# A hybrid decoder layer on one core: squares behind the rounded tiles of x, heads' rows by DMA and one transpose, the normalised input split in place

## The reference, cut to what matters

```
h = rmsnorm(x) * g_mix
proj = h @ w_in + b_in      # cv, cg (512 each), q, k, v, og (1024 each), ig, fg (4 each), ga, gb (1024 each)
a = cv * sigmoid(cg);  c = silu(layernorm(depthwise31(a)));  conv_out = c @ w_co
log_i = ig;  log_f = log_sigmoid(fg)
# mLSTM per head (4 heads of 256), by chunks, with a running maximum m:
#   bcum = cumsum(log_f); D = bcum[t] - bcum[s] + log_i[s]; m_t = max(bcum + m, max D)
#   weights exp(D - m_t), inter exp(bcum + m - m_t), states decayed by exp(bcum_end + m - m_new)
mlstm = sigmoid(og) * headnorm(h_heads) * g_mn
x = x + (sigmoid(ga) * conv_out + sigmoid(gb) * mlstm) @ w_o
x = x + (silu(gt) * up) @ w_fo      # gt, up = split(rmsnorm(x) * g_ffn @ w_fi)
y = rmsnorm(x) * g_final            # and the new conv rows and states C, n, m
```

## Time and profile before

| | us |
|---|---|
| median of 3 runs | 962.69 |
| lowest, highest | 961.84, 964.0 |
| the profiled execution, its own time | 963.81 |
| its span, first to last instruction | 962.3 |
| TensorE busy in it | 940.0 |
| VectorE, ScalarE, GpSimd busy | 774.7, 466.4, 120.2 |
| mean granted TensorE clock | 0.989 of full speed |

### The profile page before, as it was taken

One profiled execution on the slowest core, in us unless ns is written; L12 is line 12 of the kernel. 1 busy time (PEld: TensorE's weight loads), 2 busy tenths in 40 slices (PEclk: granted clock), 3 DMA queues, 4 the chain that ended last, 5 costly groups with the idle time before them and its releaser, 6 DMA issues.

```text
span 962.3 us, 18468 instructions
## 1 busy us (share of the span) xinstructions
PE 940.0 (98%) x6846; PEld 914.1 (95%) x6846; DVE 774.7 (81%) x1231; ACT 466.4 (48%) x686; POOL 120.2 (12%) x117
## 2 busy tenths in 40 slices
PE   6999999999999999999999999999999999999996
PEld 5999999999999999999999999999999999999995
DVE  6875979698779859796445559899888998989996
ACT  5743454246344524453743344455445554555573
POOL 4133051015003300510123000000000000000001
PEclk9988999999999999999999999999999999999998
DMA  5225212620442152123242222222232223233122
GB/s 194 86 66 175 72 41 100 219 87 23 156 161 66 55 219 88 44 87 138 97 162 67 86 88 88 88 89 90 96 121 91 88 66 111 90 108 109 48 86 98
DMA packets 22067, 97.26 MB, mean 101 GB/s; under 512 B 2704, under 2 KB 4880, under 8 KB 17648
## 3 DMA queue, kind: packets, MB, share of 16 engines
q1 hardware_dynamic: 19504, 77.13, 24.3%
q0 software_dynamic: 1680, 18.42, 5.2%
q10 hardware_dynamic: 816, 0.88, 0.3%
HBM read 84.03 MB, written 12.39 MB: 100 GB/s over the span
## 4 chain that ended last, share of the span: by engine, by line
PE 81%; DVE 9%; issue 3%; ACT 3%; DMA 1%; POOL 1%; SPq 0%; POOLq 0%; DVEq 0%; ACTq 0%
PE ps L1286 43%; PE ps L1558 25%; PE ps L1531 3%; PE ps L1386 2%; PE ps L1410 2%; PE ps L1458 2%; DMA raw<-w_fp_in 1%; PE ps L1396 1%; DVE main L2156 1%; PE ps L1467 1%; DVE hf L1743 1%; PE ps L1443 1%; PE ps L1447 0%; DVE main L2189 0%; PE ps L1445 0%
## 5 line engine op out<-in xcount | busy, mean ns | idle before, releaser
L1286 PE MATMUL ps<-h_hi,w_hi 128*128 128x288 f32 x896 | 194.9, 299 | 0.0
L1286 PE MATMUL ps<-h_lo,w_hi 128*128 128x288 f32 x896 | 192.7, 297 | 0.0
L1286 PE MATMUL ps<-h_hi,w_lo 128*128 128x288 f32 x896 | 192.5, 297 | 0.0
L785 ACT ACTIVATE w_hi<-raw 128x1024 fp32r<-128x1024 f32 x76 | 80.3, 1057 | 186.7 <-PE ps L1286 184.0
L1286 PEld LDWEIGHTS ps<-h_hi,w_hi 128*128 128x128 f32 x896 | 144.3, 190 | 2.1 <-issue 1.4
L1286 PEld LDWEIGHTS ps<-h_hi,w_lo 128*128 128x128 f32 x896 | 145.2, 190 | 0.0
L1286 PEld LDWEIGHTS ps<-h_lo,w_hi 128*128 128x128 f32 x896 | 145.1, 190 | 0.0
L1681 DVE TENSOR_TENSOR w_lo<-raw,w_hi 128x1024 fp32r<-128x1024 f32 x76 | 94.2, 1239 | 58.0 <-ACT w_hi L785 57.8
L1896 DVE SCALAR_TENSOR_TENSOR conv<-a_p,vec,conv x120 | 97.6, 813 | 0.2
L721 POOL TENSOR_TENSOR cs_lo<-cs,cs_hi 128x512 fp32r<-128x512 f32 x32 | 42.3, 1356 | 166.4 <-ACT cs_hi L921 166.4
L1558 PE MATMUL ps<-cols_b,late 128*128 128x288 f32 x432 | 62.8, 294 | 0.0
(11 more groups left out here) (360 smaller groups left out, 1886.9 us busy)
## 6 DMA issues: line engine op xcount, KB each, us to landing
raw<-w_head_in SPq DMA_DIRECT2D x40, 512.0 KB, 3.5
raw<-w_fp_in SPq DMA_DIRECT2D x18, 1024.0 KB, 4.8
cs<-st_c_in POOLq DMA_DIRECT2D x4, 2048.0 KB, 9.3
c_s_out<-cs POOLq DMA_DIRECT2D x4, 2048.0 KB, 7.7
raw<-w_fo_in SPq DMA_DIRECT2D x8, 1024.0 KB, 4.8
x<-xT_in SPq DMA_DIRECT2D x16, 288.0 KB, 4.2
raw<-w_cgcv_in SPq DMA_DIRECT2D x8, 512.0 KB, 4.7
raw<-w_ga_in SPq DMA_DIRECT2D x8, 512.0 KB, 3.6
```

The costliest lines, as they stand in the source:

```text
L785: act.activation(w_hi[:, s, :], raw[:, s, :], ACT.Copy).then_inc(hi_ready, 1)
L1286: last = pe.matmul(ps[:, 2 * s + b, 0:HALF], wt[:, w, k * P:k * P + P], src[:, k, b * HALF:b * HALF + HALF], start=(k == 0 and wt is w_hi ...
```

## The change

1. **Squares.** All eight tiles of x are rounded first; the eight squares follow, to `xsq`, which lies over the space of `h_hi` and `h_lo`, and VectorE alone adds them. The first weights are loaded ahead of the second tile of x. `mean` moves from the end of unit 0 to the middle of unit 1. The first table that ScalarE loads is that of the square root.
2. **First pair.** ScalarE copies units 0 and 1 out of PSUM unscaled (`unscaled`); VectorE scales them in place later (`scaled_there`). The split of unit 2's weights stands ahead of the reciprocal.
3. **Heads' rows.** `nrow`, `drow` and `rows` go to DRAM by GpSimd's DMAs. `nrow` and `drow` come back spread over all partitions, to `negm` and `dec`; `rows` comes back as `items`, 88 partitions of 128, and one transpose in the middle of unit 7 turns it. `sel`, `keep_negm` and TensorE's small products go.
4. **Normalised input.** VectorE writes `hn` (all eight tiles, in the space of `h_lo`) and subtracts in place to `h_lo`. TensorE waits for each tile of it inside the head's first unit.

```diff
@@ names and places @@
+        xsq = nc.alloc_sbuf_tensor_at("xsq", [P, KT, T], F32, offset=place[0])
         h_hi = sb("h_hi", [KT, T], F32R)
+        hn = nc.alloc_sbuf_tensor_at("hn", [P, KT, T], F32, offset=place[0])
         h_lo = sb("h_lo", [KT, T], F32R)
-        sel = sb("sel", [NH, P], parts=NH)
+        items = sb("items", P, parts=NH * NI)
@@ SyncE @@
-            sp.dma_start(x[:, 1, :], xT[:, 1, :]).then_inc(x_loaded[1], 16)
             sp.dma_start(raw[:, 0, :], w_cgcv[0]).then_inc(raw_loaded[0], 16)
-            for k in range(2, KT):
+            for k in range(1, KT):
@@ GpSimd @@
-            for k in range(KT):
-                pool.wait_ge(hhi_ready, k + 1)
-                pool.tensor_tensor(h_lo[:, k, :], hf[:, k % 2, :], h_hi[:, k, :].bitcast(F32), ALU.subtract)\
-                    .then_inc(hlo_ready, 1)
-
-            pool.wait_ge(mrow_ready, 1)
+            pool.wait_ge(mrow_ready, 2)
+            pool.dma_start(nrow_d, nrow[:, :]).then_inc(negm_spread, 16)
             pool.dma_start(m_p, mrow[:, TP - 1:TP]).then_inc(out_stored, 16)
+            pool.wait_ge(negm_spread, 16)
+            pool.dma_start(negm[:, :, :], nrow_d.partition_broadcast(P)).then_inc(negm_spread, 16)
             pool.wait_ge(exps_in, 1)
             pool.dma_start(m_s, mend[:, :]).then_inc(out_stored, 16)
+            pool.wait_ge(exps_out, 4)
+            pool.dma_start(rows_d.rearrange("(h n) p -> h (n p)", h=NH), rows[:, :]).then_inc(items_moved, 16)
+            pool.dma_start(drow_d, drow[:, :]).then_inc(negm_spread, 16)
+            pool.wait_ge(items_moved, 16)
+            pool.dma_start(items[:, :], rows_d).then_inc(items_moved, 16)
+            pool.wait_ge(negm_spread, 48)
+            pool.dma_start(dec[:, :, :], drow_d.partition_broadcast(P)).then_inc(negm_spread, 16)
+            pool.wait_ge(negm_spread, 64)
@@ ScalarE @@
-                if k >= 2:
-                    act.wait_ge(sq_added_odd if k % 2 else sq_added, k // 2)
-                act.activation(tmp[:, k % 2, :], x[:, k, :], ACT.Square).then_inc(sq_ready, 1)
...
+            for k in range(KT):
+                act.activation(xsq[:, k, :], x[:, k, :], ACT.Square).then_inc(sq_ready, 1)
+
+            def unscaled(u):
+
+                act.wait_ge(unit_done, u + 1)
+                act.activation(halves(conv if u else tmp, 0), slot(u), ACT.Copy).then_inc(slot_read[u], 1)
...
-            deviation(3, sum_done, 1)
-
             act.wait_ge(gates_done, 1)
...
             split_hi(1, 0)
+            unscaled(0)
+            deviation(3, sum_done, 1)
+            unscaled(1)
+            split_hi(1, 1)
             conv_gate(0)
-            split_hi(1, 1)
@@ TensorE @@
-            pe.wait_ge(slot_read[2], 1)
-            pe.wait_ge(exps_out, 4)
-            pe.wait_ge(masks_ready, 2)
-            for n in range(NI):
-                pe.transpose(ps[:, 4, n * NH:n * NH + NH], rows[:, n * P:n * P + P], ident[0:NH, 0:NH])
...
-            pe.wait_ge(hlo_ready, KT)
+            def turn_items(k):
+                if k == KT // 2:
+                    pe.wait_ge(slot_read[2], 1)
+                    pe.wait_ge(items_moved, 32)
+                    pe.wait_ge(masks_ready, 2)
+                    pe.transpose(ps[:, 4, 0:NH * NI], items[:, :], ident[0:NH * NI, 0:NH * NI]).then_inc(turned, 1)
+
+            unit(N_A - 1, 1, 1, C_B - 1, xg_hi, xg_lo, KT, ready=turn_items)
...
+                head_unit(0, beside=lambda k: pe.wait_ge(hlo_ready, k + 1))
@@ VectorE @@
-                if k % 2 == 0:
-                    add_square(k)
-            dve.wait_ge(sq_added_odd, KT // 2)
-            dve.wait_ge(sq_added, KT // 2)
-            dve.tensor_tensor(acc[:, :], acc[:, :], hf[:, 0, :], ALU.add).then_inc(sq_added, 1)
             split_lo(1, 1)
+            for k in range(1, KT):
+                add_square(k)
...
+            split_lo(2, 0)
             rstd(3, 1, 1)
             dve.wait_ge(rs_ready, 1)
-            scaled(0)
-            split_lo(2, 0)
-            scaled(1)
+            scaled_there(0)
             split_lo(3, 1)
+            scaled_there(1)
...
+            def normalised_lo(k):
+
+                dve.wait_ge(hhi_ready, k + 1)
+                dve.tensor_tensor(h_lo[:, k, :], hn[:, k, :], h_hi[:, k, :].bitcast(F32), ALU.subtract)\
+                    .then_inc(hlo_ready, 1)
```

More of the change, by code:

```diff
@@ L853, in _ @@
             conv_gate(2)
-            for k in range(5):
+            for k in range(4):
                 norm_hi(k)
             split_hi(3, 1)
-            for k in range(5, KT):
+            for k in range(4, KT):
                 norm_hi(k)
-            split_hi(4, 0)
+                if k == KT - 3:
+                    split_hi(4, 0)
             conv_gate(3)
-            def keep_negm(h):
-                act.wait_ge(negm_spread, h + 1)
-                act.activation(halves(negm, h), slot(3 - h % 2), ACT.Copy).then_inc(slot_read[3 - h % 2], 1)
-            keep_negm(0)
             split_hi(4, 1)
-            for h in range(1, NH):
-                keep_negm(h)
             def evac_bias(h, j, dst):
@@ L1325, in _ @@
             unit(0, 0, 0, START, xg_hi, xg_lo, KT, ready=beside_first_unit)
-            unit(1, 1, 1, START, xg_hi, xg_lo, KT)
+            unit(1, 1, 1, START, xg_hi, xg_lo, KT, ready=beside_second_unit)
             with pe.Fori(1, N_A // 2 - 1) as i:
@@ L1330, in _ @@
             unit(N_A - 2, 0, 0, C_B - 1, xg_hi, xg_lo, KT)
-            pe.wait_ge(slot_read[2], 1)
-            pe.wait_ge(exps_out, 4)
-            pe.wait_ge(masks_ready, 2)
-            for n in range(NI):
-                pe.transpose(ps[:, 4, n * NH:n * NH + NH], rows[:, n * P:n * P + P], ident[0:NH, 0:NH])
-            for h in range(NH):
-                last = pe.matmul(ps[:, 5, h * SB:h * SB + SB], sel[:, h, :], drow[:, :], start=True, stop=True)
-            last.then_inc(turned, 1)
-            for h in range(NH):
-                s = 3 - h % 2
-                pe.wait_ge(slot_read[s], (1 if s == 3 else 2) + h // 2)
-                for b in range(2):
-                    last = pe.matmul(ps[:, 2 * s + b, 0:HALF], sel[:, h, :], nrow[:, b * HALF:b * HALF + HALF],
-                                     start=True, stop=True)
-                last.then_inc(negm_spread, 1)
-                if h == 0:
-                    unit(N_A - 1, 1, 1, C_B - 1, xg_hi, xg_lo, KT)
-            pe.wait_ge(hlo_ready, KT)
+            def turn_items(k):
+                if k == KT // 2:
+                    pe.wait_ge(slot_read[2], 1)
[3 more added lines that the diff above has]
+            unit(N_A - 1, 1, 1, C_B - 1, xg_hi, xg_lo, KT, ready=turn_items)
             with pe.Fori(0, NH) as h:
@@ L1375, in read @@
                         pe.wait_ge(dve_read, h * DVE_USES + (READER[:k].count("dve") + START + 1))
-                for j in range(6):
+                head_unit(0, beside=lambda k: pe.wait_ge(hlo_ready, k + 1))
+                for j in range(1, 6):
                     head_unit(j)
@@ L1836, in _ @@
             split_lo(6, 0)
-            for k in range(5):
+            for k in range(4):
                 normalised(k)
+                if k:
+                    normalised_lo(k - 1)
             scaled(5)
+            normalised_lo(3)
             split_lo(7, 1)
+            for k in range(4, KT):
+                normalised(k)
+                if k == KT - 2:
+                    scaled(6)
+                    split_lo(8, 0)
+                if k > 4:
+                    normalised_lo(k - 1)
+            normalised_lo(KT - 1)
             conv_input(2)
-            for k in range(5, KT):
-                normalised(k)
-            scaled(6)
-            split_lo(8, 0)
             dve.wait_ge(turned, 1)
-            steps.on(dve.tensor_copy(dec[:, :, :].rearrange("p h b -> p (h b)"), ps[:, 5, 0:NH * SB]))
-            dve.tensor_copy(cols[:, :, :].rearrange("p i h -> p (i h)"), ps[:, 4, 0:NI * NH]).then_inc(slot_read[2], 1)
+            dve.tensor_copy(cols[:, :, :], ps[:, 4, 0:NH * NI].rearrange("p (h i) -> p i h", h=NH))\
+                .then_inc(slot_read[2], 1)
             dve.wait_ge(slot_read[2], 2)
```

70 lines of the change are left out of this document (35 added, 35 removed).

## The result

| | before | after |
|---|---|---|
| median of 4 runs each, us | 963.35 | **951.41** |
| lowest, highest | 961.84, 965.13 | 950.99, 951.82 |
| profiled execution, its span | 963.81, 962.3 | 951.21, 949.7 |

The ratio is 0.9872, with a 95% interval of 0.9855 to 0.9888: 11.9 us faster by the medians, 12.6 in the two profiled executions. The forecast was 13.8, and 948.9 us for the median. 951.41 lies 2.5 above that, outside the forecast's own range (947.5 to 950.4) and inside the wider one (947.0 to 953.0). Of the 2.5 us, 0.66 is the median of the kernel before, which is 963.35 over four runs and was 962.69 over three.

The account below looks back on a forecast made before the run. TensorE, busy 940.0 of 962.3 us, bounds the kernel; thin work and slow clock cost 13.6. Head 0's first unit moves from 81.31 to 70.2, its second from 90.36 to 76.6: 962.69 - 13.8 = 948.9, range 947.0 to 953.0.

Parts of the forecast that it names:

- Thin work and slow clock: TensorE, 64.03 to 90.36: small work of 4.3 + 4.1 us and slow clock of 2.5 + 2.7 go, 13.6 together.
- The DMA chain: Heads' rows through DRAM to `items`: there at 60 us, needed at about 66.9 inside unit 7, cover 7 us.
- "DVE blocks DMA": VectorE's two-port instructions stop GpSimd writing descriptors: four DMAs 10 us later, 3 over the cover, 952 to 955.
- The low end: Cheapest DMA chain after the exponentials end at 54.1: two round trips with two issues, 4.8 us, given as 59.4.
- VectorE's steps: Splitting h on VectorE: steps of 0.73, 0.67 and 1.13 us, 7.5 from first product to unit 7's weights at 63.7.
- Rival 2: VectorE dearer than counted, beside GpSimd's descriptor writing or with gaps: up to 3.4 us, 951 to 952.3; chance 0.07.
- The start: Gates' chain on VectorE 0.5 to 0.6 us later; unit 2 at 30.0 instead of 32.04; unit 5 waits 1.8.
- The price of a fall of the clock: Two slow stretches on TensorE lasted 6.6 and 6.4 us; at half speed 3.4 us of work lost.
- rivals 1, 3 and 4: Clock falls in unit 5's wait, 952.3 (0.12); DMA chain late, 959.3 (0.03); chain over 23.2 us, slower, 965.5 (0.03).
- rivals 1 and 2: Clock falls in unit 5's wait, 952.3 (0.12); VectorE dearer than counted, 951 to 952.3 (0.07).
- 11.8 us against 12.9 of TensorE: VectorE's work up to the weights of the head's unit 1 takes 11.8 us, covered by TensorE's 12.9.
- The sum: Whole kernel: gain of 13.8 us, 950.0 for the profiled execution and 948.9 for the median; chance 0.70.

Follow-up runs that it names:

- the long chain: The changed kernel with three more round trips of the heads' rows through DRAM in GpSimd's queue; 964.05 us, ratio 1.0003.

## Point by point: why the prediction was right, and its 1.9 us

- **Thin work and slow clock**: forecast 13.6 less 0.15. Measured: 13.5 us less of busy TensorE, the granted clock recorded at 1.00 without a break until 939.0 us. Right, and the runs with one part alone show that it takes both parts.
- **The DMA chain**: `items` taken at 60, measured 60.9 (58.36, and 2.5 to landing); needed at 66.9, measured 66.79 with no wait ahead. One more trip is hidden, three are not.
- **"DVE blocks DMA"**: the estimate by the Trainium skill's warning was 10 us of delay. The low end itself was added up wrong (54.1 + 4.8 is 58.9, not 59.4); `items` landed 2.0 us behind it. No such delay is in these traces: GpSimd's issues took 0.69 for the first and 0.51 to 0.57 for the others. Beside the issues of the long chain VectorE ran products and subtractions; what a copy there would have done, no run shows.
- **VectorE's steps**: 0.73, 0.67 and 1.13 from start to start; `w_lo` of unit 7 done at 63.7, measured 63.45. Rival 2 did not happen.
- **The start**: gates' row at 34.3, measured 33.96; unit 5's wait 1.8, measured 1.46, ending at 50.6 (50.95); the head's first unit 70.08 (70.2). The account is right, and that it came this close is in part luck: in equal code `mean` alone starts anywhere between 25.2 and 26.5 (last section).
- **The price of a fall of the clock**: 3.4 us in rivals 1, 3 and 4, taken from stretches of 6.5 us that held the thin work too. The prediction's own rows gave 2.5 and 2.7 us for a unit, and the two falls that the runs forced cost 2.4 each. None of this entered the forecast. The measured time lies nearest to what rivals 1 and 2 gave (951 to 952.3), but neither of them happened in this kernel.
- **The step that failed**: "11.8 us against 12.9 of TensorE. So 1.1 us of cover is left." The sum counts `cols` and its followers with 1.6 us; they took 3.8 (71.90 to 75.70), since one of the copies was held by GpSimd's filling for 2.1 us more than its own time. 2.2 us more, less the cover of 1.1, are the wait of 1.17; the second unit started at 77.65 instead of 76.6. Moving either the copies or the filling gives 1.65 to 2.1 us back, of which the wait explains 1.17. The prediction looked at what GpSimd's queue waits for and whom it holds up, and not at whom it disturbs once it runs.
- **The end**: TensorE is 13.1 us earlier at the first of the last products (936.80 against 949.91), the span 12.6 shorter. The last spreading products took 3.87 instead of 2.73, as the granted clock fell at 939.0, at their start, and before only at 954.1. The half us between the two differences arises behind that point, and I take these products for its cause. It is not the change's own: the same products took 2.46 to 4.18 in the other kernels.
- **The sum**: in the profiled executions 12.6 and the 1.17 of the collision are 13.8. By the medians, the two kernels without the collision are 13.9 (the copies moved) and 14.0 (the filling moved) below the kernel before in their own groups. So the collision is what separates 11.9 from 13.8, as far as medians that vary by 0.5 us can tell.

## What to carry over

When a step is taken off the busiest engine and given to two others, add up what the second of them then does *at the same moment* as the first: two instructions that wait last for the same event will run side by side. Ask also which wait was the last before: here the removed `negm` copies had kept the filling away from VectorE's copies. And where two edits remove two causes of the same slow stretch, measure them together; alone they gave 6.0 of the 11.3 us.

## What the runs showed of the hardware that I had not expected

- GpSimd filled `qm` (128 x 2176, 1.92 us) beside a copy of 32 x 4 float32 on VectorE, and the copy took 2.29 us instead of 0.16. A subtraction of 128 x 1024 beside the same filling stayed at 1.21.
- TensorE's granted clock stayed at full speed through an idle time of 1.46 us. It fell to 0.50 within those of 5.08, 6.26 and 12.25 us and was still there when the work came back: behind the wait of 5.08 until 5.7 us after it, behind that of 12.25 until 4.8 us after it.
- The first matmuls run at half the later pace, though the granted clock is recorded as 1.00 there, and for how long differs in equal code: pairs were 0.48 us apart until 14.2 in the changed kernel and until 15.7 with the filling moved. In six kernels with the same instructions up to `mean`, it started between 25.2 and 26.5 us. A difference of up to 1.3 us between single profiles says nothing unless it is taken behind that point.
